# Two of three score products of the second attention by one 128-row matmul a head

## The reference

```python
def even_mixer(h, w_in, q_gain, k_gain, sink, w_out, rope1, rope_axial):
    qa, ka, va, qb, kb, vb = jnp.split(h @ w_in, cuts, axis=-1)
    qa = apply_axial_rope_2(rms_norm_2(qa, q_gain), *rope_axial)   # 8 heads of 64
    ka = apply_axial_rope_2(rms_norm_2(ka, k_gain), *rope_axial)   # 2 heads
    oa = global_gqa(qa, ka, va)
    qb = apply_rope(qb, *rope1)                                    # 8 heads
    kb = apply_rope(kb, *rope1)                                    # 2 heads
    ob = windowed_gqa_sink(qb, kb, vb, sink)
    return jnp.concatenate([oa, ob], axis=-1) @ w_out
```

## Time and profile before

| what | value |
|---|---|
| time, median of 3 runs | 2486.62 us (2485.47 to 2487.55) |
| the profiled execution's own time | 2488.92 us |
| its span, first to last instruction | 2487.1 us |
| mean granted TensorE clock | 0.995 |
| PE busy | 2438.2 us, 98% |
| POOL busy | 1641.4 us, 66% |
| DVE busy | 1097.6 us, 44% |
| ACT busy | 668.1 us, 27% |

### The profile page before, as it was taken

The page is one execution under the profiler, slowest core; times in us unless marked ns, Lnnn a source line. Parts: engine busy times, 40 slices in busy tenths (PEclk is TensorE's granted clock), DMA queues, the critical chain, the costliest instruction groups (busy, mean ns, idle before and its releaser), DMA issues.

```text
span 2487.1 us, 32523 instructions
## 1 busy us (share of the span) xinstructions
PE 2438.2 (98%) x11606; PEld 1976.4 (79%) x11606; DVE 1097.6 (44%) x1465; ACT 668.1 (27%) x1252; POOL 1641.4 (66%) x1432
## 2 busy tenths in 40 slices
PE   6999999999999999999999999999999999999998
PEld 4886678888888887778888888888888777888886
DVE  4455644454433227765333223334226566433311
ACT  4264521122111106652111111111112674211100
POOL 3545946666666776546676776666777765666775
PEclk9999999999999999999999999999999999999999
DMA  7313632333333332003332333323333221323332
GB/s 269 115 60 136 203 110 94 96 98 93 98 96 96 106 103 91 24 18 104 95 99 93 102 108 95 101 93 98 105 101 106 88 71 61 98 95 98 97 102 84
DMA packets 68947, 248.57 MB, mean 100 GB/s; under 512 B 7424, under 2 KB 9984, under 8 KB 68224
## 3 DMA queue, kind: packets, MB, share of 16 engines
q1 hardware_dynamic: 63808, 232.81, 29.5%
q10 hardware_dynamic: 5056, 14.64, 1.6%
HBM read 245.32 MB, written 2.10 MB: 99 GB/s over the span
## 4 chain that ended last, share of the span: by engine, by line
PE 95%; DVE 2%; ACT 1%; DMA 1%; POOL 1%; issue 1%; DVEq 0%; ACTq 0%; SPq 0%; POOLq 0%
PE pb L576 74%; PE pb L1165 4%; PE pb L1105 2%; PE pb L861 2%; PE pb L1029 2%; PE pb L585 1%; PE pb L744 1%; PE pb L1011 1%; PE pb L1148 1%; PE pb L995 1%; PE pb L1133 1%; PE pb L1121 1%; PE pb L788 1%; PE pb L1181 1%; PE pb L812 1%; PE pb L775 1%
## 5 line engine op out<-in xcount | busy, mean ns | idle before, releaser
L576 PE MATMUL pb<-ar,w_hi 128*128 128x512 f32 x5312 | 1642.7, 390 | 0.9 <-POOL w_lo L407 0.6
L576 PEld LDWEIGHTS pb<-ar,w_hi 128*128 128x128 f32 x5312 | 994.2, 188 | 218.1 <-issue 8.0
L576 PE MATMUL pb<-ar,w_lo 128*128 128x512 f32 x2656 | 1033.7, 389 | 0.0
L407 POOL TENSOR_TENSOR w_lo<-raw,w_hi 128x1024 fp32r<-128x1024 f32 x379 | 950.1, 2507 | 31.7
L576 PEld LDWEIGHTS pb<-ar,w_lo 128*128 128x128 f32 x2656 | 498.5, 188 | 104.9
L404 POOL TENSOR_TENSOR still<-still 128x1 f32<-128x1 f32 x392 | 81.1, 207 | 692.2 <-PE pb L576 546.6
L405 POOL TENSOR_SCALAR w_hi<-raw 128x1024 fp32r<-128x1024 f32 x379 | 402.7, 1063 | 0.0
L2077 DVE TENSOR_TENSOR tb<-pb,nb 128x512 f32<-128x512 f32 x88 | 60.9, 692 | 400.8 <-PE pb L576 400.8
L2083 DVE TENSOR_TENSOR ar<-tb,ar 128x512 f32 x88 | 156.2, 1775 | 90.9 <-ACT ar L1492 90.9
L1492 ACT ACTIVATE ar<-tb 128x512 f32 x88 | 55.7, 633 | 512.7 <-DVE tb L2080 512.7
L1974 DVE SCALAR_TENSOR_TENSOR x<-pb,x 128x512 f32<-128x512 f32 x48 | 36.2, 757 | 347.5 <-PE pb L576 343.0
(11 more groups left out here) (263 smaller groups left out, 2402.0 us busy)
## 6 DMA issues: line engine op xcount, KB each, us to landing
raw<-wstream SPq DMA_DIRECT2D x427, 512.0 KB, 3.5
raw<-wstream SPq DMA_DIRECT2D x4, 1024.0 KB, 10.7
x<-xt ACTq DMA_DIRECT2D x2, 2048.0 KB, 10.2
tb<-wstream SPq DMA_DIRECT2D x2, 1024.0 KB, 11.7
rt<-wstream SPq DMA_DIRECT2D x2, 1024.0 KB, 12.0
out<-x ACTq DMA_DIRECT2D x8, 256.0 KB, 2.6
rt<-nbias ACTq DMA_DIRECT2D x4, 384.0 KB, 3.8
nb<-nbias ACTq DMA_DIRECT2D x4, 384.0 KB, 3.5
```

Of the source, the lines that this page charges most:

```text
L407: pool.tensor_tensor(lo, src, hi.bitcast(F32), ALU.subtract).then_inc(s_split, 1)
L576: mm = pe.matmul(pb[:, bank, :], weights(a, n, t)[:, k * P:(k + 1) * P], rhs(b, k0 + k), start=(first and k == 0 and i == 0), stop=(last a ...
```

## The change

High and low query rows of one head now lie on top of each other, and so one matmul over 128 rows gives high x high plus low x high for it. `E_Q[g][side]` and `E_K[g][side]` are indexed by the head's side instead of the part. For side 0 the high query rows are on partitions 0 to 63 and the low ones on 64 to 127; for side 1 the other way round. `E_K[g][side]` holds the high keys of that side in both halves. The low keys of both sides lie in a new tile `E_KL[g]`, in a part of `Y2` that is written only at the end of the attention. A unit's scores are two matmuls of 128 rows (one a side), then two of 64 rows, high query by low key.

To fill this, the high part of a query tile is two copies of 64 rows instead of one of 128, that of a key tile four; the low part is two subtractions of 64 rows instead of one, for queries with a result on the other half than its inputs. The functions `stacked_hi` and `stacked_lo` take the places of `qk_hi_part` and `qk_lo_part` in the stage even2 and wait for the same semaphores. The first attention keeps the old ones.

```diff
--- before.py
+++ after.py
@@ -159,6 +159,16 @@
                  for o in (8192 + 6144 * g + 5120, 20480 + 1024 * g)] for g in range(2)]
         E_PT = [[area(4096 * b + 2048 * s, 4, TOK) for s in range(2)] for b in range(2)]
         Y2 = [area(22528 + 4096 * s, KT, TOK) for s in range(2)]
+
+        E_KL = [Y2[g][:, 7, :] for g in range(2)]
+
+        def query_or_key(m):
+
+            if m in (4, 5):
+                return [E_K[m - 4][side] for side in range(2)]
+            return [E_Q[m // 6][side][:, m % 6, :] for side in range(2)]
+
+        SIDES = (slice(0, 64), slice(64, 128))
 
         O_V = ar[:, 8192:17408].rearrange("p (z k q c) -> p z k q c", z=18, k=4, q=2)
         O_Y = [[ar[:, 8192 + 1024 * hp + TOK * s:8192 + 1024 * hp + TOK * (s + 1)] for hp in range(KT)] for s in range(2)]
@@ -989,14 +999,12 @@
                 elif w >= 18:
                     pe.wait_ge(bt["mx"], w - 1)
                 lo, hi = (0, 4) if g == 0 else (chunks_of(j)[0], chunks_of(j)[-1] + 1)
-                for q, (a, b) in enumerate(PASSES):
-                    for side in range(2):
-                        rows = slice(64 * side, 64 * side + 64)
-                        mm = pe.matmul(pb[:, S_BANKS[w % 2][side], 0:(hi - lo) * P],
-                                       E_Q[g][a][rows, i, j * P:(j + 1) * P], E_K[g][b][rows, lo * P:hi * P],
-                                       start=(q == 0), stop=(q == 2))
-                        if q == 2:
-                            mm.then_inc(bt["s"], 1)
+                for side in range(2):
+                    pe.matmul(pb[:, S_BANKS[w % 2][side], 0:(hi - lo) * P], E_Q[g][side][:, i, j * P:(j + 1) * P],
+                              E_K[g][side][:, lo * P:hi * P], start=True, stop=False)
+                for side, rows in enumerate(SIDES):
+                    pe.matmul(pb[:, S_BANKS[w % 2][side], 0:(hi - lo) * P], E_Q[g][side][rows, i, j * P:(j + 1) * P],
+                              E_KL[g][rows, lo * P:hi * P], start=False, stop=True).then_inc(bt["s"], 1)
 
             def turn_b(w):
                 g, i, j = pair_b(w)
@@ -1497,9 +1505,16 @@
             ffn("ffn0")
 
 
-            dest = {0: E_Q[0][0][:, 0, :], 1: E_Q[0][0][:, 1, :], 2: E_Q[0][0][:, 2, :], 3: E_Q[0][0][:, 3, :],
-                    4: E_K[0][0], 5: E_K[1][0], 6: E_Q[1][0][:, 0, :], 7: E_Q[1][0][:, 1, :],
-                    8: E_Q[1][0][:, 2, :], 9: E_Q[1][0][:, 3, :]}
+            def stacked_hi(m):
+
+                act.wait_ge(s_qm, 12 + m + 1)
+                to = query_or_key(m)
+                for side, rows in enumerate(SIDES):
+                    ins = act.activation(to[side][rows, :], tb[rows, 4, :], ACT.Copy)
+                    if m in (4, 5):
+                        ins = act.activation(to[side][SIDES[1 - side], :], tb[rows, 4, :], ACT.Copy)
+                ins.then_inc(s_qhi, 1)
+
             c = 12
             for m in range(10):
                 act.wait_ge(s_group, SPL0["even2"] + m + 1)
@@ -1507,7 +1522,7 @@
                     qk_square(c, m % 4)
                 qk_rotate(c, m % 4)
                 if m > 0:
-                    qk_hi_part(c - 1, dest[m - 1])
+                    stacked_hi(m - 1)
                 if CALLS[c][2] is not None:
                     qk_root(c)
                 if m == 0:
@@ -1515,7 +1530,7 @@
                     act.wait_ge(s_qrs, 2 * calls_before(c, "norm") + 2)
                     norm_rstd("n3", 5, dst=acc)
                 c += 1
-            qk_hi_part(21, dest[9])
+            stacked_hi(9)
 
             wm = nb[:, 1, 0:3 * P]
             act.dma_start(wm, wmask).then_inc(s_ld["wmask"], 16)
@@ -2088,9 +2103,15 @@
             ffn("ffn0")
 
 
-            dest = {m: [E_Q[0][s][:, m, :] for s in range(2)] for m in range(4)}
-            dest.update({4: E_K[0], 5: E_K[1]})
-            dest.update({6 + m: [E_Q[1][s][:, m, :] for s in range(2)] for m in range(4)})
+            def stacked_lo(m):
+
+                dve.wait_ge(s_qhi, 12 + m + 1)
+                of = query_or_key(m)
+                for side, rows in enumerate(SIDES):
+                    to = E_KL[m - 4][rows, :] if m in (4, 5) else of[side][SIDES[1 - side], :]
+                    ins = dve.tensor_tensor(to, tb[rows, 4, :], of[side][rows, :].bitcast(F32), ALU.subtract)
+                ins.then_inc(s_qlo, 1)
+
             def v_copy(i):
                 dve.wait_ge(s_group, SPL0["even2"] + 11 + i)
                 dve.tensor_tensor(tb[:, 6 + i, :], pb[:, 2 + i, :], acc, ALU.mult).then_inc(s_ev, 1)
@@ -2102,11 +2123,11 @@
                     dve.wait_ge(s_table, 2)
                 if m == 10:
                     v_copy(0)
-                    qk_lo_part(21, *dest[9])
+                    stacked_lo(9)
                 else:
                     qk_gain(c, m % 4)
                     if m > 0:
-                        qk_lo_part(c - 1, *dest[m - 1])
+                        stacked_lo(m - 1)
                     qk_done(c, TILE0["even2"] + m + 1)
                     c += 1
                 if m in (1, 2):
```

## The result

| | before | after |
|---|---|---|
| time, median of 4 runs each | 2486.05 us (2484.70 to 2487.55) | 2497.57 us (2496.51 to 2499.17) |
| the profiled execution's own time | 2488.92 us | 2498.22 us |
| its span | 2487.1 us | 2496.3 us |
| mean granted TensorE clock | 0.995 | 0.994 |

The account below looks back on a forecast made before the run. PE, busy in 98% of the span, was taken to bound the kernel. Scores 0 plus projection and handover +10.2 on the 2486.62 us median gave 2496.8 us; own range 2493.3 to 2500.3, extended to 2491.0 and 2500.5 towards the rivals.

Parts of the forecast that it names:

- The scores: Score units of the second attention: six 64-row matmuls already cost three slots, so no change, bounds -3.5 to +3.5 us.
- The mark of 0.89 us per unit: Check on the score units: PE still needs 0.89 us from a unit's first matmul to the next operation.
- The loop: ACT and DVE loop in the projection's early tiles: added copies and subtractions delay the squares, and PE loses 3.9 us.
- the walk: Tile-by-tile tracing of added copies and low parts through projection and handover, giving +10.2 us at PE.
- the second is inside L405 and is held to 956.1: Tile 1 of the projection: POOL's split holds the second low part, so square 3 comes late and PE loses 1.9 us.
- Tile 3: Projection step: second low part held to 964.5, square 4 3.9 us late; called close, 0.9 less if not held.
- never ends inside one of POOL's weight splits: Projection: a DVE instruction with two SBUF inputs that meets POOL's split ends 0.55 us after POOL does.
- the third rival: Projection tiles 6 to 9: DVE holds up POOL, weights come late and PE waits; +4, 2500.8 us, chance 0.07.
- Key tiles and handover: From tiles 4 and 5 on, DVE's lag stays; L978 waits for v's copy, PE +9.8; under 8 would refute the step.
- Alternating halves: Low parts switching partition halves on DVE might lose their 0.08 us overlap; sum about 10.6, left out of the forecast.
- The first (halves not held by POOL, +3.0): Rival in the projection: half-height low parts escape POOL's hold and the lag melts before the handover; 2489.6 us, chance 0.13.
- The second (faster): Rival in the score units: weights load unseen and 0.11 us goes in 32 units; -3.5, 2483.1 us, chance 0.03.

## Why the prediction was right, and where its steps were not

**The scores: right.** Zero was forecast, 0.5 us was measured, in the traces of after and of the run with the old fill alike. The mark of 0.89 us per unit failed in the letter: it is 0.99, with a start 0.09 sooner. That the pairs of 64 rows already ran side by side, six in three slots, decided it.

**The loop: right kind, mis-sized (2.4 for 3.9).** Up to the low parts of tile 1 the walk fits: counted on the clock of before, L1862 ends at 952.64 (forecast 952.6) and the low parts start at 953.98 and 954.68 (953.95 and 954.55). Then the step that failed: "the second is inside L405 and is held to 956.1". DVE and POOL of after:

```profile
952.67 1.39 DVE L2112 TENSOR_TENSOR ar<-tb,ar 64x512 fp32r<-64x512 f32 x2
954.09 0.69 DVE L1842 SCALAR_TENSOR_TENSOR nb<-pb,tb 128x512 f32<-128x512 f32 x1
...
953.38 1.60 POOL L415 TENSOR_SCALAR w_hi<-raw 128x1024 fp32r<-128x1024 f32 x1
...
960.26 1.39 DVE L2112 TENSOR_TENSOR ar<-tb,ar 64x512 fp32r<-64x512 f32 x2 [0.33 <-ACT ar L1513]
...
960.98 1.59 POOL L415 TENSOR_SCALAR w_hi<-raw 128x1024 fp32r<-128x1024 f32 x1
```

The second low part of tile 1 started at 953.37, 0.01 us ahead of L415, that of tile 2 (the one under "Tile 3") at 960.96, 0.02 ahead, and it was POOL that waited: 1.60 for 1.05. The first square so held up came 0.65 earlier than forecast, PE's waits at L736 were 1.12 and 0.98 instead of 1.9 each. The prediction had called the second of them close and priced it at 0.9; both were close, and neither was held.

Behind it stands a reading that was too wide: "never ends inside one of POOL's weight splits". That holds for a DVE instruction that starts inside one. In the kernel before, at the end of the projection, one that starts first ends inside, and the split is the longer one (DVE, POOL):

```profile
995.25 0.91 DVE L1854 TENSOR_TENSOR ar<-tb,ar 128x512 fp32r<-128x512 f32 x1
...
995.71 2.71 POOL L407 TENSOR_TENSOR w_lo<-raw,w_hi 128x1024 fp32r<-128x1024 f32 x1
```

L1854 ends at 996.16, and L407 takes 2.71 for 2.40. The L407 of 2.98 us in the earlier trace rows, which the third rival names, is the same thing.

**Key tiles and handover: right.** The first low parts of tiles 4, 6, 7 and 8 start in L417 and end 0.55 behind it, as the walk had it; that of tile 5, which it had held too, starts 0.1 us ahead of the end of L417 and is not. Again on the clock of before, the sum of tile 5 was 7.2 late (forecast 8.3), that of tile 6 8.6 (9.6), that of tile 9 8.7 (9.8), and L988 came 8.7 late (9.8). All four lack the same 1.0 to 1.1, most of the 1.5 that the loop did not cost. From the last L736 to L988 alone the forecast was 5.9, the trace has 6.3. L988 is more than 8 us late, as the step asked, but its own wait is 3.6 and not "some 5": 1.9 was already waited ahead of the scores, where the walk had 1.5, and the scores, for the most part at half clock, took 1.64 us for the 1.16 they take at full clock (in the run with v copied early). What the walk did not say, and the runs did, is that the 6.3 are in the main one whole turn of POOL (5.44) and a second low part (0.7; with one low part a tile 5.5 are left of the 6.3), and that small parts decide whether the turn is lost.

**What came on top: missing.** The clock's fall, 2.1 us by the run with spare matmuls, was no term of the sum. Of the 0.2 to 0.4 that the sum had behind L988, the same run shows 0.24. The clock (+2.1), the units (+0.5) and the handover (+0.4) stand against the 1.5 that the loop did not cost, so that the sum, 10.2, came within 1.3 of the 11.5 measured. That two errors of opposite sign met is luck; the total was better than its terms.

**Alternating halves.** Low parts on alternating halves stand 0.70 apart (960.26 with x2 in 1.39), and the operation behind them another 0.72 (961.68), where the earlier trace rows had 0.60 start to start. So the hold of the Trainium skill ("VectorE: DVE Perf Modes", Two Vector instructions with no wait between them) is borne out, some 0.1 us a time. The operation behind writes where the second low part of a query tile wrote; what changes there is where the inputs start, which the same section of the Trainium skill names as well. What these tenths cost in the total no run here separates. ACT's copies on alternating halves are 0.64 apart as well (copies of 64 rows at 991.13 and 991.77), dearer than the 0.58 of the estimate; by the prediction's own test such a difference moves the sum by some tenths.

**The rivals.** The first (halves not held by POOL, +3.0) is nearly what the kernel with its result in PSUM is, for tiles 4 to 9: it is 3.5 us slower than before by the medians, 4.3 by the traces. So the forecast and this rival differed in the hold alone, as was said. The second (faster) found nothing. The third (POOL held by DVE) had its mechanism, L415 at 1.60, but no delay: the chain of after has POOL at 1% as before, and PE waits nowhere in this stage for weights.

## What to carry to other kernels

Stacking two products of 64 rows into one of 128 rows saves nothing where the 64-row products already run in pairs: count slots of the array, not matmuls. Where an engine competes with another's periodic, exclusive work, the question is not how much is added but whether the next instruction still starts ahead of the period; measure that margin (0.45 us here). Beyond it one small part costs nearly the whole lag and a second one little more; below it the lag is made up. Keep one input of such instructions in PSUM where a bank is free. And price an idle stretch of PE at a stage's border with what the granted clock does behind it.

## What the hardware showed that was not expected

- The hold between DVE and POOL works both ways and by who starts first: a start 0.01 us ahead of L415 (tile 1 of after) cost POOL 0.55 us and DVE nothing.
- After PE had been nearly idle from 995 to 1002.5, the granted clock was 0.50 for the first 5 us of work, and about 2.1 us were lost there. With a wait of 0.95 us ahead of the turn of v (the kernel with its result in PSUM) it stayed at 1.00, and so it did with a wait of 1.92 us ahead of the scores when 8 us of work without a break came behind it (v copied early). The moment of the fall is not set by the waits alone: with the old units, after the same first wait, it came at about 1001 and not at 998.
- Going from a pair of 64 rows back to 128 rows costs 0.43 us to the next start here and 0.32 before, after the same pair. Ahead of that pair stands 128-row work now and stood another pair before; why that should matter stays open.
